# A two-layer mixture-of-experts encoder on one core: from four experts at a time to one

## The reference

```python
pg = softmax(x2 @ w_rg + b_rg); p_top, g_sel = top_k(pg, 1)     # 4 groups
le_sel = (x2 @ w_re + b_re).reshape(T, 4, 8)[arange(T), g_sel]
v2, i2 = top_k(softmax(le_sel), 2)                              # 2 of 8 experts
gate = p_top * v2 / sum(v2)
h = silu(xb @ w_gate[e]) * (xb @ w_up[e])                       # w_gate, w_up: 1024 x 512
y[token] += gate * (h @ w_down[e])                              # w_down: 512 x 1024
```

## Time and profile before

| | |
|---|---|
| median of 3 runs | 1231.53 us (1229.88 to 1232.38) |
| the profiled execution | 1234.95 us, span 1233.2 us |
| busy share of the span | PE 73%, PE weight load 31%, VectorE 16%, ScalarE 12%, GpSimd 3% |
| HBM read | 437.34 MB, 356 GB/s over the span |
| chain that ended last | DMA 52%, PE 39%, SyncE's queue 3%, VectorE 2% |
| mean granted TensorE clock | 0.867 of full speed (2.4 GHz) |

### The profile page before, as it was taken

How to read it: one execution, slowest core, us unless ns; L and a number is a source line. 1 busy time by engine, 2 the same in 40 slices (tenths; PEclk the granted TensorE clock), 3 DMA queues, 4 the chain that set the end, 5 groups by cost and what they waited for, 6 DMA issues and landing times.

```text
span 1233.2 us, 12289 instructions
## 1 busy us (share of the span) xinstructions
PE 895.3 (73%) x4789; PEld 377.2 (31%) x4789; DVE 203.4 (16%) x541; ACT 143.7 (12%) x326; POOL 35.4 (3%) x43
## 2 busy tenths in 40 slices
PE   6998886766675666576799989985756665665655
PEld 3453532222131312131354454431312121222211
DVE  1133311101010101010220261320101010101101
ACT  1031310000000000000120270310000000000000
POOL 3311000000000000000000010000000000000000
PEclk9998999688788878887999889997878788878888
DMA  9963679999999999999963326699999999999995
GB/s 276 356 260 137 234 299 420 421 423 422 421 422 422 423 421 422 422 422 421 392 225 137 122 84 239 273 422 421 421 423 421 422 422 423 421 422 421 423 421 232
DMA packets 72807, 438.73 MB, mean 356 GB/s; under 512 B 7544, under 2 KB 7664, under 8 KB 23632
## 3 DMA queue, kind: packets, MB, share of 16 engines
q1 hardware_dynamic: 70896, 434.51, 86.4%
q0 software_dynamic: 1088, 2.97, 1.0%
q10 hardware_dynamic: 800, 0.94, 0.3%
HBM read 437.34 MB, written 1.05 MB: 356 GB/s over the span
## 4 chain that ended last, share of the span: by engine, by line
DMA 52%; PE 39%; SPq 3%; DVE 2%; issue 2%; ACT 1%; DVEq 0%
PE psum L1180 38%; DMA ring<-in_moe_w_down 26%; DMA ring<-in_moe_w_gate 24%; SPq L419 3%; DMA ring<-in_ev_w_in 2%; PE psum L1187 1%; ACT phase L632 0%; DVE phase L1170 0%; DVE phase L981 0%; DVE phase L985 0%; PE psum L1389 0%; DVE x L788 0%; ACT phase L590 0%; ACT phase L725 0%; DVE phase L883 0%
## 5 line engine op out<-in xcount | busy, mean ns | idle before, releaser
L1180 PE MATMUL psum<-ring,phase 128*32 128x512 f32 (+1 forms) x3072 | 510.0, 754 | 267.1 <-DMA ring<-in_moe_w_down 92.7
L1180 PEld LDWEIGHTS psum<-ring,phase 128*32 128x32 f32 (+1 forms) x3072 | 148.3, 138 | 586.8 <-issue 571.9
L1180 PE MATMUL psum<-ring,scratch 128*128 128x512 f32 x320 | 145.7, 616 | 5.7 <-DMA ring<-in_ev_w_in 5.4
L1180 PE MATMUL psum<-phase 128*128 128x512 f32 (+4 forms) x416 | 113.8, 499 | 17.2 <-DVE phase L925 14.4
L1180 PEld LDWEIGHTS psum<-ring,scratch 128*128 128x128 f32 x320 | 62.8, 199 | 84.2 <-issue 76.6
L1180 PEld LDWEIGHTS psum<-phase 128*128 128x128 f32 (+3 forms) x416 | 50.6, 171 | 71.7 <-issue 65.5
L1180 PEld LDWEIGHTS psum<-phase,xs 128*128 128x128 f32 x512 | 60.7, 195 | 9.5 <-issue 8.4
L1180 PE MATMUL psum<-phase,xs 128*128 128x128 f32 x512 | 61.7, 279 | 0.9 <-DVE phase L867 0.9
L923 DVE TENSOR_TENSOR phase<-psum,phase 128x512 f32<-128x512 f32 x16 | 11.1, 692 | 293.4 <-ACT phase L596 293.4
L925 DVE COPY phase<-psum 128x512 f32<-128x512 f32 x16 | 11.1, 692 | 279.6 <-PE psum L1180 279.6
L929 DVE TENSOR_TENSOR x<-x,psum 128x512 f32<-128x512 f32 x64 | 44.0, 688 | 28.7 <-PE psum L1180 28.7
(11 more groups left out here) (158 smaller groups left out, 378.7 us busy)
## 6 DMA issues: line engine op xcount, KB each, us to landing
ring<-in_moe_w_up SPq DMA_DIRECT2D x124, 1024.0 KB, 16.7
ring<-in_moe_w_down SPq DMA_DIRECT2D x124, 1024.0 KB, 19.9
ring<-in_moe_w_gate SPq DMA_DIRECT2D x120, 1024.0 KB, 18.5
ring<-in_od_w_in SPq DMA_DIRECT2D x6, 2048.0 KB, 19.9
ring<-in_ev_w_in SPq DMA_DIRECT2D x3, 2048.0 KB, 32.2
ring<-in_ev_w_out SPq DMA_DIRECT2D x2, 2048.0 KB, 25.6
scratch<-in_moe_w_gate SPq DMA_DIRECT2D x4, 1024.0 KB, 10.8
phase<-in_moe_w_gate SPq DMA_DIRECT2D x4, 1024.0 KB, 6.0
```

Source lines behind the costliest of these rows:

```text
L1180: return nc.tensor.matmul(out_, lhsT, rhs, start=start, stop=stop)
```

## The change

It takes one expert at a time. Each matrix is one slot and one transfer, with runs of 4096 floats (16 KB) a partition. The 32 columns of the array that an expert had are now column groups g of one expert: for gate and up, group g holds 128 columns of both (one moving side of 2 x 128); for down, 256 output columns (`COLS`). hT comes from a VectorE transpose in place of four PE transposes. x is put into PSUM banks 0 to 3 ahead of the routing (in place of the `WARM` matmuls), and `combine` adds each expert's result onto it there: eight matmuls for every expert, whose inputs lie on 32 partitions of their own each. Only at the end of a layer x is copied back, by ScalarE and VectorE. The scaling of x moves into the 0/1 matrix (now `Ss`), and `gather` reads x with a step of 8 floats; `xs`, `scratch`, `lcst` and `phase` are gone, and all the work memory lies in the eleven slots of one tensor `mem` and in a small area. Experts 0 to 30 are written out; expert 31, and any second rounds, run in a loop at the middle of the layer (`LOOP_AT` = 16). The constants of layer 1 are loaded when B has ended, and no more when A has.

```diff
-DN_PIECES = FF // P
-ITEM = GU_PIECES + DN_PIECES
-SLOTS = 6
-WARM = 4
+SLOTS = 11
 SLOT = 4096
-EXTRA = 4
+PIECES = 3 * EXPERTS
+LOOP_AT = EXPERTS // 2
+STATIC = EXPERTS - 1
...
-        ring = sb("ring", SLOTS * SLOT)
+        mem = sb("mem", SLOTS * SLOT + AREA)
-        xs = sb("xs", TT * D)
-        scratch = sb("scratch", SLOT)
...
+        DENSE = {"A": (0, 1, 2, 3, 8, 9), "C": (8, 9, 10, 0, 1, 2, 7, 8)}
+        RING = {"B": tuple(range(SLOTS)), "D": (9, 10, 0, 1, 2, 4, 6, 5, 7, 8, 3)}
...
+            def load(l, kind, e, to):
+                name, rows = (("moe_w_gate", DC), ("moe_w_up", DC), ("moe_w_down", DN_ROWS))[kind]
+                return sp.dma_start(to.rearrange("p (e f) -> p e f", e=1),
+                                    a[name][l, bass.ds(e, 1)].rearrange("e (p r) f -> p e (r f)", r=rows))
...
+            for n in range(PIECES):
...
+                if n < 4:
+                    sp.wait_ge(used["A"], n + 1)
+                elif n == 4:
+                    sp.wait_ge(s_qms, 1)
+                elif n == 5:
+                    sp.wait_ge(s_sc, HP)
+                    sp.wait_ge(s_f2, 4)
+                elif n < 8:
+                    sp.wait_ge(s_o, HP)
+                elif n < 10:
+                    sp.wait_ge(used["A"], n - 3)
+                elif n == 10:
+                    sp.wait_ge(used["A"], n_a)
+                else:
+                    sp.wait_ge(used["B"], n - SLOTS + 1)
+                expert_piece("B", 0, n)
...
+                if n < 5:
+                    sp.wait_ge(used["C"], n + 2)
+                elif n == 5:
+                    sp.wait_ge(s_nu, HEADS)
+                    sp.wait_ge(s_dl, HEADS)
+                elif n == 6:
+                    sp.wait_ge(s_hTp, 4)
+                elif n == 7:
+                    sp.wait_ge(s_hn, 2 * HEADS)
+                elif n < 11:
+                    sp.wait_ge(used["C"], 7 if n == 8 else 8)
...
-            pool.wait_ge(used["A"], n_a)
-            pool.dma_start(lcst[:, :], a["c_layer1"]).then_inc(s_load["lc1"], 16)
+            pool.wait_ge(used["B"], PIECES)
+            pool.dma_start(C["lcst"], a["c_layer1"]).then_inc(s_load["lc1"], 16)
...
+                def select(q):
+                    for t in range(TT):
+                        for k in range(QUAD):
...
+                            ins = V.tensor_scalar(Ss_m[:, t, k], slotid[:, 0:CAP], rk3[:, t, e:e + 1], inv_rms(t),
+                                                  ALU.is_equal, ALU.mult)
...
-                for _ in range(WARM):
-                    mm(bank(6), ident, x[:, 0:512])
+                for g in range(QUAD):
+                    total_g, x_g = acc(g)
+                    last = mm(total_g, ident, x_g)
...
+                def gather(out_, c, rhs):
+                    for t in range(TT):
+                        last = mm(out_, x3[:, t, c::DC], rhs[t], t == 0, t == TT - 1)
+                def gate_up(g_slot, u_slot, k, ready=None):
+                    for r in ORDER_R:
...
+                        for g in range(QUAD):
+                            w = g_slot[:, r * FF + g * P:r * FF + (g + 1) * P]
...
+                            last = mm(bank(4)[g * CAP:(g + 1) * CAP, 0:2 * P].rearrange("p (j n) -> p j n", j=2),
+                                      xT_m[:, r, k * CAP:(k + 1) * CAP], both, r == ORDER_R[0], r == ORDER_R[-1])
+                def down(d_slot):
+                    for r in range(DN_ROWS):
+                        for g in range(QUAD):
+                            last = mm(bank(5)[g * CAP:(g + 1) * CAP, 0:COLS], hT_m[:, r, :],
+                                      d_slot[:, r * D + g * COLS:r * D + (g + 1) * COLS], r == 0, r == DN_ROWS - 1)
+                def combine(half_done=None):
+                    for t in range(TT):
+                        for g in range(QUAD):
+                            last = nc.tensor.matmul(bank(g)[:, t * COLS:(t + 1) * COLS], M["GT"][g * CAP:(g + 1) * CAP, t * P:(t + 1) * P],
+                                                    M["y"][g * CAP:(g + 1) * CAP, :], start=False, stop=True,
+                                                    skip_group_check=True)
...
+                for e in range(STATIC):
...
+                    gate_up(piece_slot(ph, n), piece_slot(ph, n + 1), k,
+                            chunk_ready if k == 0 else None).then_inc(used[ph], 5 if e == LOOP_AT else 2)
+                    if e not in (0, LOOP_AT):
+                        pe.wait_ge(s["y"], e)
+                        pe.wait_ge(s["gtc"], e)
+                        combine()
+                    pe.wait_ge(s["gsel"], 2 * (e + 1))
+                    gates_T().then_inc(s["gtp"], 1)
+                    if k == QUAD - 1 and e + 1 != LOOP_AT:
+                        gather_quad(q + 1)
+                    pe.wait_ge(*arrived[ph, n + 2])
+                    pe.wait_ge(s["hT"], e + 1)
+                    down(piece_slot(ph, n + 2)).then_inc(used[ph], 1)
```

More of the change, by code:

```diff
@@ new lines, in last_and_more @@
+            def last_and_more(ph, l):
+                s = ms[l]
+                n0 = 3 * LOOP_AT
+                sp.wait_ge(used[ph], n0 + 3 - SLOTS)
+                sp.wait_ge(s["rounds"], 1)
+                extra = sp.value_load(extra_i[0:1, l:l + 1], min_val=0, max_val=EXPERTS * (MAX_ROUNDS - 1))
+                with sp.Fori(0, extra + 1) as i:
+                    e = sp.snap((i + STATIC) % EXPERTS)
+                    sp.wait_ge(s["more_slots"], i + 1)
+                    sp.sem_inc(s_free, 1)
+                    for kind in range(3):
+                        load(l, kind, e, piece_slot(ph, n0 + kind)).then_inc(s["more_landed"], 16)
@@ L609, in _ @@
+                act.wait_ge(s["done"], 1)
+                for g in (1, 3):
+                    total_g, x_g = acc(g)
+                    nc.scalar.copy(x_g, total_g).then_inc(s["final_a"], 1)
             norm(0)
@@ new lines, in moe @@
+                for e in range(STATIC):
+                    q, k = divmod(e, QUAD)
+                    if e == LOOP_AT:
+                        last_and_more()
+                        select(q)
+                        select_gates(e)
+                    if k == 0 and q:
+                        copy_chunks(q)
+                    gated(bank(4)[:, P:2 * P], s["silu"], e + 1, s["hT"])
+                    if e + 1 < STATIC and e + 1 != LOOP_AT:
+                        dve.wait_ge(s["gtp"], e + 1)
+                        select_gates(e + 1)
+                    if k == 1 and q + 1 < QUADS and e + 3 != LOOP_AT:
+                        select(q + 1)
@@ new lines, in gather_quad @@
+                def gather_quad(q):
+                    pe.wait_ge(s["sel"], 2 * (q + 1))
+                    for half in (1, 0):
+                        if half == 0 and q:
+                            pe.wait_ge(s["gtc"], QUAD * q)
+                        for c in range(4 * half, 4 * half + 4):
+                            last = gather(bank(6 + half)[:, c % 4 * P:(c % 4 + 1) * P], c,
+                                          [M["Ss"][:, t * P:(t + 1) * P] for t in range(TT)])
+                        last.then_inc(s["disp"], 1)
@@ L1322, in _ @@
+                pe.wait_ge(s["y"], STATIC)
+                pe.wait_ge(s["gtc"], STATIC)
+                combine().then_inc(s["done"], 1)
             pe.wait_ge(s_load["cst"], 16)
```

551 lines of the change are left out of this document (252 added, 299 removed).

## The result

The changed kernel takes **1222.61 us** (1221.46 to 1223.81, 4 runs) beside 1231.01 of the kernel before on the same chip: ratio 0.9931, 95% interval 0.9914 to 0.9949. It is faster, by 8.4 us where 23.2 were forecast. Over all experiments the executions of the kernel before fall into two groups, 1228 to 1233 and 1234 to 1237 us, and its profiled execution (1234.95) is one of the upper. Mixer A has 2.5 of the difference between the profiles: `x_T` of B starts at 137.01 us after and at 139.56 before. That is no gain of the change: in the 13 profiles of the changed kernel and its variants, whose mixer A is the same, `x_T` of B starts anywhere from 135.2 to 141.8.

A forecast was written before the change was run, and what follows sets the result against it. Transfers were taken to bound the MoEs. Per layer −4.97 (piece), −6.4 (rate), +1.7 (first slot) made −9.7; both −19.4, tails −3.9: −23.2, so 1208.3 us beside the median (1211.7 as profiled), range 1195 to 1227.

The forecast's parts named there:

- Strided reads: Gather's loads of x with a step of 32 bytes: taken as no change; if doubled, first slot 6.7 us late.
- Rival 2: Gathers slow down by their step: 10 us more, 1218.3 us; chance 0.10.
- The sign of being wrong: Start of the MoE: forecast wrong if the 32 gather records take over 8 us.
- First slot back: MoE start, through select, gathers and gate_up: first slot returned at 163.3 us, 1.7 later than before.
- Rate: Expert transfers in 16 KB runs: 428.5 GB/s, 4.89 us a piece instead of 4.97, 6.4 us less a layer.
- One more piece ahead: All eleven slots full before routing ends, leaving 85 pieces instead of 86: 4.97 us less a layer.
- In the stream: Mid-layer PE work per expert, 7.9 us against 14.7 us of transfers: hidden; combine 1.2 us.
- Rival 3: PE becomes the bound through slower gate_up and down: each layer 13 us longer, 1257 us; chance 0.12.
- The tails: After the last landing: 9.0 us in B, 1.6 less; 9.0 plus 2.9 for stores in D, 2.3 less.

The follow-up runs named there:

- e2: Changed kernel whose gather reads 128 neighbouring columns of x instead of every eighth (output not the reference's): 1215.34 us.
- e1: Changed kernel with each expert matrix loaded by two 1 MB transfers in runs of 8 KB: 1235.76 us.
- e3: Changed kernel with piece 10 of either layer held back until the first gate_up has ended: 1232.82 us.
- e7: Changed kernel with twelve more matmuls of 512 columns for two of every four experts, 4 to 27, in each layer: 1222.36 us.
- e9: Changed kernel with x written back in column order, plus 3,500 written-out GpSimd semaphore counts from D's first gather, touching no memory: 1227.88 us.
- e10: Changed kernel with x written back in order, plus written-out semaphore counts on ScalarE, VectorE and TensorE for experts 4 to 27, both layers: 1226.36 us.
- e12: Changed kernel with x in order and five filler matmuls before the last written-out gate_up; experts 4 to 27 omit some matmul rows, all transfers kept: 1206.48 us.
- e5: Changed kernel with x written back in order, plus 3,500 one-column GpSimd memsets from D's first gather on, which nothing waits for: 1231.65 us.

## Why the prediction was wrong

The mechanism was right where the gain comes from: the stream bounds the MoE, and the longer runs and the eleventh piece brought nearly what was forecast. What failed is the price: two costs were put at nothing, the strided weight loads and the code reads. The MoEs gave 10.8 us in the profiles where 23.3 were forecast for them. The 12.5 us between are 8.2 of strided loads, 6.4 of code reads and what may stand beside them, and 2.8 of rate, less 2.6 at the first slot of B and 2.3 in the tails. The measured 1222.6 lies inside the range (1195 to 1227), but the range did not reach up for the code: it had no term for it.

- **Strided reads, "I take no change": this is the step that failed.** The argument was that the loads are by another engine than ScalarE and that the MATMUL records overlap them. They overlap, but the load is the longer of the two, so it sets the pace. Without the step the start of each layer is 4.1 us shorter (e2), and the median 7.3. ScalarE's two rows, 2140 against 1051, were the right guide: the factor is the same. Rival 2, given 0.10, is what happened, at 7.3 in place of 10. The Trainium skill (SBUF — State Buffer, Door 1: the DMA port swizzle) had the rule; the trace agrees with it now. The sign of being wrong, over 8 us for the 32 records, was set on a base that was too long: 5.9 us in order, where e2 shows 3.84. So the doubled loads came to 7.89 and passed just under it.
- **First slot back, +1.7.** Without the step (e2) the start is 21.2 us in both layers: 0.9 less than before in B, 1.7 more in D. In B the terms were too dear by 2.6: gathers 3.84 for 5.9, `gate_up` 3.66 for 4.3, against select's 1.75 for 1.5. In D the forecast is met by luck. It was worked out for B and used for both, but D was already 2.6 us shorter before, with PE at full clock: its gathers and `multiply` took

```profile
780.49 2.05 PE L1180 MATMUL psum<-phase,xs 128*128 128x128 f32 x16 [0.47 <-DVE phase L867]
...
783.76 3.64 PE L1180 MATMUL psum<-ring,phase 128*32 128x512 f32 x32 [1.22 <-DVE phase L883]
```

  where B's took 3.22 and 5.12. One layer's row stood for two, and the two errors cancelled there. With the strided loads the start measured +3.2 in B (1.7 − 2.6 + 4.1) and +5.8 in D (1.7 + 4.1).
- **Rate, 428.5.** It measured 427 (4.91 us a piece, not 4.89): 1.4 short a layer, within the bounds. e1 shows that the length of the runs makes it: 6.1 a layer in the stream, somewhat more than from 422 to 427, since e1 ran at 420 to 421.
- **One more piece ahead, −4.97.** Right: 5.1 a layer (e3).
- **In the stream.** Right that all of it is hidden (e7), though PE waits for a quarter of the time and not for nearly half: the gathers take twice as long, and the granted clock was 0.84 in both long stretches. `combine` 1.08 to 1.15 for 1.2. Rival 3 falls: 16 groups of 256 columns take 3.66, so half the columns take half the time.
- **A term that wasn't in the sum: code reads.** Before, 86 × 4.97 and a rest of 4.2 us make the stream of 431.6. After, 84 pieces of 4.91 to the last `w_up` and the same 4.2 would make 416.7; it measured 419.9. The 3.2 more are the steps. This is the second cost that was put at nothing, and the prediction doesn't mention it. Writing the experts out (19,625 instructions for 12,289) put 0.9 MB more of instruction reads on the DMA engines that bring the weights. That is 0.2% of the bytes, but not spread over all 16 engines: eight are behind at the end, and PE's last wait ends with the slowest. e9 and e10 lengthen the stream with code that nothing waits for, e12 shortens it by 1.8 a layer with 0.2 MB less. An estimate from the rows agrees: 70 packets of q8 are 0.4% of 16 engines' time over 1219.7 us, 1.1 us each; 29 of them fall into the stream of B where before had 3, and 26 × 1.1 over eight engines is 3.6 us. For e12, with 17, it gives 1.7 less. That all 3.2 are code was not shown: no version with as little code as before was tried.
- **The tails, −1.6 and −2.3.** From the last wait's end B took 12.3 us, D 16.1 to the end of the span; less the 4.9 that the last `gate_up` starts ahead of the last landing, 7.4 and 11.2 for 9.0 and 11.9 forecast. A little better than forecast.

So in B: 4.1 − 2.6 at the start, 1.4 of rate, 3.2 of steps, −1.6 in the tail: 4.5 of the 4.4 missing. In D: 4.1 + 1.4 + 3.2 − 0.7 = 8.0 of 8.1. Mixer C is unchanged. The 13.5 us between the two profiled executions are 10.8 from the MoEs, 2.5 of mixer A and 0.2 of C. The medians stand 8.4 apart; of the 5.1 between, 2.5 are mixer A's, which varies by more than that from profile to profile, and where the rest fell can't be told from one profile each.

## What to carry to other kernels

Where a kernel is at the rate of its transfers, price everything by what it does to the moment when the stream starts for good and to its slowest DMA engine. Read a weight load's step before calling it free, and let an engine that is idle there lay the data out in the order of the reads. Read a start or a tail in each layer, since the clock and so the base can differ; and count instructions when a loop is written out, since code comes over the same DMA engines as the data.

## What the runs showed of the hardware

- TensorE's weight loads of 128 float32 columns take 199 ns on the mean in order and 334 with a step of 32 bytes (e2); with the longer loads a gather record took 0.247 us, with the shorter 0.12.
- Runs of 16 KB gave 427 GB/s, of 8 KB 422 (420 to 421 in e1), of 2 KB 387. The 358 GB/s that the Trainium skill (DMA: Bandwidth & Descriptors, Where 436 GB/s comes from) has for one core's reads did not bind here.
- Instruction reads cost stream time out of proportion: 0.23 MB for GpSimd 11.9 us (e9), as one DMA engine ended some 12 us behind the rest while the mean rate in mid-layer stayed at 426. Each packet of 8 KB put that engine 0.6 to 0.7 us further behind, and it did not catch up within the layer. The Trainium skill (Runtime: NRT & Kernel Launch, Instruction fetch mechanics) says that each engine fetches its code in blocks of 16 KB through a DMA queue of its own and that this is mostly hidden. The 70 packets and 1.15 MB of q8 agree with the size; q14's packets were of 8 KB. No wait of PE for its code shows in the changed kernel, but the transfers pay for it.
- A chain can name "another core or an unknown queue" where the wait is an ordinary one. Two such stretches of D, the first here, are waits of PE for `w_up` in its own timeline, and the increments of these transfers end at the same times (1129.6 and 1144.3 us); a third, in B (516.30, 6.91 us), is the same. They are no waits for code:

```profile
1121.95 7.66 another core or an unknown queue
```

```profile
1129.75 5.09 PE L1218 MATMUL psum<-mem 128*32 128x256 f32 x64 [7.80 <-DMA mem<-in_moe_w_up]
...
1144.43 5.83 PE L1218 MATMUL psum<-mem 128*32 128x256 f32 x56 [6.29 <-DMA mem<-in_moe_w_up]
```

- Beside a row of small GpSimd memsets one VectorE operation lasted 6.99 us in place of 0.17, and two further ones 6.22 together in place of 0.60 (e5).
